# A two-block layer in fp32 on one core: the mixer loop rewritten with 64x64 TensorE tiles, scales in tables, and a planned order for each engine

## What is computed

```
# gated delta rule: 4 heads of 128, the sequence in chunks
kk   = k k^T;   lmat = dec_strict * kk * beta          # strictly lower triangular
sol  = solve(I + lmat, [v, gam * k])                    # unit lower triangular
attn = dec_incl * (q k^T) * beta
# step over the chunks:  u = u_v - w_k S;  o = q_dec S + attn u;  S = g_end S + k_end^T u
o_a  = rmsnorm(o) * gdn_norm_w * silu(z)
# dilated attention: 8 heads of 64, three (window, step) patterns merged into one softmax
p = exp(q k^T + log(number of patterns that hold the pair) - max);  o_b = (p v) / sum(p)
```

## Time and profile before

| what | value |
|---|---|
| time, median of 3 runs | 2759.99 us (2754.16 to 2760.57) |
| time of the profiled execution | 2761.34 us |
| span of its profile | 2759.7 us, granted TensorE clock 0.975 |
| DVE, ACT, POOL busy over the span | 57%, 38%, 6% |
| PE instructions in the mixer loop | 2896 |

### The profile page before, as it was taken

How to read it: one execution, slowest core, us unless ns; L and a number is a source line. 1 busy time by engine, 2 the same in 40 slices (tenths; PEclk the granted TensorE clock), 3 DMA queues, 4 the chain that set the end, 5 groups by cost and what they waited for, 6 DMA issues and landing times.

```text
span 2759.7 us, 33118 instructions
## 1 busy us (share of the span) xinstructions
PE 2632.9 (95%) x12696; PEld 2164.5 (78%) x12696; DVE 1561.2 (57%) x2392; ACT 1060.4 (38%) x1602; POOL 156.2 (6%) x189
## 2 busy tenths in 40 slices
PE   6999979999899999999999999988999999999997
PEld 5878767777777878888878888876888788888886
DVE  4123325555553666666565895456488854755555
ACT  3123323333432453444554444344434333433332
POOL 1000011111220000110000000000000000000000
PEclk9999988999999999999999999999999999999999
DMA  5222230100103445556553456442322333333331
GB/s 193 94 77 87 75 113 16 39 27 27 39 16 107 131 157 192 192 193 203 192 168 92 145 183 191 132 127 69 101 86 89 92 100 92 92 122 99 92 106 62
DMA packets 318304, 304.29 MB, mean 110 GB/s; under 512 B 10207, under 2 KB 277588, under 8 KB 318036
## 3 DMA queue, kind: packets, MB, share of 16 engines
q1 hardware_dynamic: 303188, 244.18, 29.7%
q0 software_dynamic: 14976, 58.20, 5.2%
HBM read 244.68 MB, written 57.67 MB: 110 GB/s over the span
## 4 chain that ended last, share of the span: by engine, by line
PE 84%; DVE 8%; ACT 3%; DMA 2%; issue 2%; SPq 0%; POOLq 0%; POOL 0%; DVEq 0%; ACTq 0%
PE PS L1854 12%; PE PS L1856 12%; PE PS L1855 12%; PE PS L1568 11%; PE PS L1678 7%; PE PS L1871 6%; PE PS L1872 6%; PE PS L1873 6%; PE PS L1786 3%; PE PS L1809 2%; PE PS L1797 1%; DVE wl L1125 1%; ACT wh L796 1%; DVE cg L1515 1%; DMA raw<-in_w_ff 1%
## 5 line engine op out<-in xcount | busy, mean ns | idle before, releaser
L1854 PE MATMUL PS<-hh,wh 128*128 128x512 f32 x1728 | 683.9, 396 | 4.2 <-DVEq L529 2.3
L1856 PE MATMUL PS<-hh,wl 128*128 128x512 f32 x1728 | 673.9, 390 | 0.0
L1855 PE MATMUL PS<-hl,wh 128*128 128x512 f32 x1728 | 673.6, 390 | 0.0
L1125 DVE TENSOR_TENSOR wl<-raw,wh 128x1024 fp32r<-128x1024 f32 x286 | 347.5, 1227 | 393.6 <-ACT wh L796 393.1
L796 ACT ACTIVATE wh<-raw 128x1024 fp32r<-128x1024 f32 x352 | 366.8, 1055 | 517.7 <-PE PS L1873 381.9
L1411 DVE TENSOR_TENSOR x<-x,PS 128x512 f32<-128x512 f32 x432 | 293.0, 684 | 182.7 <-PE PS L1873 181.8
L1854 PEld LDWEIGHTS PS<-hh,wh 128*128 128x128 f32 x1728 | 325.1, 188 | 76.7 <-issue 4.6
L1855 PEld LDWEIGHTS PS<-hl,wh 128*128 128x128 f32 x1728 | 325.2, 188 | 70.9 <-issue 4.6
L1856 PEld LDWEIGHTS PS<-hh,wl 128*128 128x128 f32 x1728 | 325.0, 188 | 68.2
L1871 PE MATMUL PS<-fh,wh 128*128 128x512 f32 x864 | 344.6, 399 | 18.8 <-DVE x L1411 11.0
L1872 PE MATMUL PS<-fl,wh 128*128 128x512 f32 x864 | 340.0, 393 | 0.0
(11 more groups left out here) (290 smaller groups left out, 2921.2 us busy)
## 6 DMA issues: line engine op xcount, KB each, us to landing
raw<-in_w_ff SPq DMA_DIRECT2D x128, 512.0 KB, 3.9
raw<-in_w_up SPq DMA_DIRECT2D x88, 512.0 KB, 4.4
wl_s<-wl POOLq DMA_DIRECT2D x66, 512.0 KB, 5.5
wl<-wl_s SPq DMA_DIRECT2D x66, 512.0 KB, 3.5
raw<-in_w_in SPq DMA_DIRECT2D x60, 512.0 KB, 3.9
raw<-in_w_down SPq DMA_DIRECT2D x44, 512.0 KB, 5.2
raw<-in_w_out SPq DMA_DIRECT2D x32, 512.0 KB, 4.2
qkvz_s<-st POOLq DMA_DIRECT2D x16, 512.0 KB, 2.9
```

The costliest lines, as they stand in the source:

```text
L1125: TTo(wls(slot), raw[:, k % 2], whs(slot).bitcast(F32), ALU.subtract).then_inc(s["w_lo"], 1)
L1854: mm(bank, wh[:, k % 4, cut], hh[:, kk, span(a_)], start=kk == 0, stop=False)
L1855: mm(bank, wh[:, k % 4, cut], hl[:, kk, span(a_)], start=False, stop=False)
L1856: last = mm(bank, wl[:, k % 4, cut], hh[:, kk, span(a_)], start=False, stop=kk == KT - 1)
```

## The change

- The work of the mixer loop is divided differently between turns. A turn c now takes 4 of the 8 query tiles (0, 3, 4, 7 or 1, 2, 5, 6) for both heads of a pair, in six steps (`steps`, `step`) of up to 512 keys each. The heads lie on partitions 0 to 63 and 64 to 127: their scores use rows 0 to 63 and 64 to 127 of the array, with banks 3 and 4, and their product with v writes columns 0 to 63 and 64 to 127 of bank 7. That product is turned round (v stationary with 64 columns, p moving with 128), so the transposed result comes out directly and "heads" goes.
- The transposes of p become matmuls with a diagonal matrix `dgt` that holds 1/sum.
- The inversion works on the two 64x64 diagonal blocks of each head (`both`): levels 0 to 5 have 8 matmuls in "cor" and 16 in "join", all with 64 rows and 64 columns; level 6 has 4 and 4. T and TT lie in one tile `TTT` with one addition for both. Level 0 becomes a level like the others.
- The lengths of q and k and the factors of the decay go into eight tables per chunk instead of four passes over data. They are applied inside other passes, with one DVE instruction for each head (`by_head`) where there was one for four heads. k and q stay as they were loaded, so the transposes "back" go. Three exponentials over the tables are added at the end of phase 1.
- GpSimd does two memsets and nothing else. `ke` and the sum of squares move to ACT (4 instructions each), `qd` and the output's scaling to DVE.
- `ORDER` and the loop over turns go. A class `Mixers` lists every stage with what it waits for and a duration, places them all by a list schedule, and each engine's program is written out in the order of that plan. qkvb and vb get a second buffer.

```
+    TILES = (4, 7, 0, 3), (5, 6, 1, 2)
...
+    BUSY = {"gc": 0.5, "kk": 0.5, "cor": 0.36, "join": 0.6, "cor6": 0.3, "join6": 0.3, "qk": 0.5, "kT": 0.5, "vT": 0.5,
+            "kS": 0.5, "u": 0.5, "o": 1.0, "SU": 0.5, "ot": 0.5, "vt": 1.0,
+            "D": 0.85, "LT": 0.85, "U": 0.38, "T": 0.7, "AT": 0.85, "v": 0.7, "qd": 0.7, "r": 0.85, "St": 0.85, "ov": 0.15, "orec": 0.15,
+            "on": 0.7, "og": 0.76, "lo": 0.7, "mx": 0.3, "dg": 0.7, "blo": 0.25,
+            "gam": 0.6, "E": 0.63, "half": 0.65, "cp6": 0.38, "ke": 0.9, "uc": 0.6, "sq": 1.5, "osd": 2.8, "oh": 0.63,
+            "vb": 1.05, "bhi": 0.25}
...
+    def place(self):
...
+            start = {stage: max(free[engine[stage[0]]], ready_at[stage]) for stage in can}
+            soonest = min(can, key=lambda stage: (start[stage], -left[stage]))
+            e = engine[soonest[0]]
+            near = [stage for stage in can if engine[stage[0]] == e and start[stage] <= start[soonest] + self.NEAR]
+            stage = max(near, key=lambda stage: (left[stage] - self.bias(stage), -rank[stage]))
+            end = start[stage] + self.busy(stage)
...
+        def step(c, j, m):
+
+            return 6 * c + (2 * j + m if j < 2 else 2 + j)
...
             def chunk(c):
+                if c >= 2:
+                    sp.wait_ge(s["og_ready"], c - 1)
                 sp.dma_start(ch[:, c % 2], qkvz_s[:, :, c * P:(c + 1) * P]).then_inc(ch_loaded[c % 2], 16)
...
+            def pair(i):
+                if i >= 2:
+                    sp.wait_ge(s["s_mm"], 12 * (i - 1))
+                sp.dma_start(qkvb[:, i % 2], qkvb_s.rearrange("p (m t) s -> p m t s", m=3)[:, :, i, :]).then_inc(pair_loaded[i % 2], 16)
...
+            nc.gpsimd.memset(G["TTf"][:], 0.0).then_inc(s["consts_set"], 1)
...
-                    if stage == "invert":
...
-                        PT(G["kd"][:], G["knT"][:], G["gam"][:], ALU.mult).then_inc(s["kqd_ready"], 1)
-                        PT(G["qd"][:], G["qnT"][:], G["gam"][:], ALU.mult).then_inc(s["kqd_ready"], 1)
-
-                        pool.wait_ge(s["eb_ready"], c + 1)
-                        PT(G["ke"][:], G["kn"][:], G["E"][:, :, P - 1:P].broadcast_to([P, GH, P]), ALU.mult)\
...
+            act.wait_ge(s["tab_dve"], 4)
+            for dst, src, sign in ((T_NGAM, T_NGC, -1.0), (T_GE, T_GE, 1.0), (T_KE, T_KE, 1.0)):
+                A(tab[:, :, dst:dst + 4], tab[:, :, src:src + 4], ACT.Exp, scale=sign).then_inc(s["tab_act"], 1)
...
+                elif name == "ke":
+                    act.wait_ge(s["kT_mm"], c + 1)
+                    if c:
+                        act.wait_ge(s["su_mm"], c)
+                    for h in range(GH):
+                        last = A(G["ke"][:, h], heads(2)[:, h], ACT.Copy, scale=tab[:, c, T_KE + h:T_KE + h + 1])
+                    last.then_inc(s["ke_ready"], 1)
...
+            TTo(ke, ge, ngc, ALU.add).then_inc(s["tab_dve"], 1)
+            dve.wait_ge(s["tab_act"], 7)
+            done(TS(ngam, ngam, -1.0, None, ALU.mult))
+            done(TTo(ke, ke, tab[:, :, T_BP:T_BP + 4], ALU.mult))
...
+            def by_head(out, in0, col, c, in1, op0, op1):
+
+                for h in range(GH):
+                    last = STT(out[:, h], in0[:, h], tab[:, c, col + h:col + h + 1], in1(h), op0, op1)
+                return last
...
+                elif name == "U":
+                    l = stage[2]
+                    dve.wait_ge(s["lev_l"], 7 * c + l + 1)
+                    if c or l:
+                        dve.wait_ge(s["lev_w"], 7 * c + l)
+                    if l < 6:
+                        TTo(G["U"][:], corner, again(lmask[:, l], GH), ALU.mult).then_inc(s["lev_u"], 1)
+                    else:
+                        TS(G["U"][64:128], corner[64:128], -1.0, None, ALU.mult).then_inc(s["lev_u"], 1)
+                elif name == "T":
...
+                        TTo(G["TTT"][:], G["TTT"][:], inverse, ALU.add).then_inc(s["lev_t"], 1)
...
+                    for e in range(2):
+                        last = TS(dgt[:, j % 2, e], ident[:], ac[:, 3, 2 * j + e:2 * j + e + 1], None, ALU.mult)
...
-                        rows_ = slice(64 * p, 64 * p + 64)
-                        for lo in range(0, n, HALF):
-                            hi = min(n, lo + HALF)
-                            last = mm(PS[:, 3 + lo // HALF, 0:hi - lo], qkvb[rows_, 0, h * P:h * P + P],
-                                      qkvb[rows_, 1, lo:hi], start=True, stop=True)
...
-                                    last = tr(PS[:, 5 + g % 2, b * P:b * P + P],
-                                              sm[:, h % 2, (b0 + b) * P:(b0 + b) * P + P], ident[:])
...
-                                    last = mm(PS[:, 7, 0:64], pt[:, g % 2, b * P:b * P + P],
-                                              vb[:, b0 + b, 64 * p:64 * p + 64], start=b0 + b == 0, stop=b0 + b == h)
...
+            def both(dst, left, right):
+
+                for h in range(GH):
+                    for r in range(2):
+                        q = slice(64 * r, 64 * r + 64)
+                        last = mm(dst(q, h), left(q, h), right(q, h), start=True, stop=True)
...
+                elif name == "cor" and stage[2] < 6:
+                    l = stage[2]
+                    if l == 0:
+                        pe.wait_ge(s["lt_ready"], c + 1)
+                        pe.wait_ge(s["s_ready"], c + 1)
+                    else:
+                        pe.wait_ge(s["lev_t"], 6 * c + l)
+                        pe.wait_ge(s["lev_u"], 7 * c + l)
+                    both(lambda q, h: corner[q, h], lambda q, h: G["LT"][q, h, q],
...
+                    back = (lambda q, h: G["TTT"][q, 1, h]) if l else unity
+                    both(lambda q, h: inverse[q, 0, h], back, lambda q, h: G["U"][q, h])
+                    both(lambda q, h: inverse[q, 1, h], lambda q, h: G["U"][q, h], back).then_inc(s["lev_w"], 1)
...
+                    for e in range(2):
+                        rows_ = slice(64 * e, 64 * e + 64)
+                        last = mm(PS[:, 3 + e, 0:hi - lo], qkvb[rows_, i % 2, 0, at:at + P], qkvb[rows_, i % 2, 1, lo:hi],
...
+                            last = mm(PS[:, 5 + e, b - lo:b - lo + P], soft(j)[:, e, b:b + P], dgt[:, j % 2, e], start=True, stop=True)
...
+                    for b in range(lo, hi, P):
+                        for e in range(2):
+                            ch_ = slice(64 * e, 64 * e + 64)
+                            last = mm(PS[ch_, 7, 0:P], vb[:, i % 2, b // P, ch_], pt[:, e, b - lo:b - lo + P], start=b == 0, stop=b + P == n)
```

More of the change, by code:

```diff
@@ L521, in program @@
         ch_loaded = [sem(f"ch_loaded{i}") for i in range(2)]
-        pair_loaded = sem("pair_loaded")
+        pair_loaded = [sem(f"pair_loaded{i}") for i in range(2)]
         out_moved = [sem(f"out_moved{i}") for i in range(4)]
@@ L540, in rows, with soft @@
             return w[bass.ds(r, P), :]
[L544 to L557, removed]
+        mixers = Mixers()
+        def step(c, j, m):
+            return 6 * c + (2 * j + m if j < 2 else 2 + j)
+        def soft(j):
+            return sm[:] if j % 2 == 0 else raw[:]
         units = [tiles_of(Dense(), b) for b in range(2)]
@@ L624, in _ @@
             chunk(1)
[L625 to L632, removed]
+            pair(1)
+            for c in range(2, TT):
+                chunk(c)
+                if c in (3, 5):
+                    pair((c + 1) // 2)
             end_phase(sp, 2)
@@ L762, in _ @@
-            turns(pool, turn)
             end_phase(pool, 2)
@@ L1378, in _ @@
[L1378 to L1380 removed]
+            ge, ke, ngam, ngc = (tab[:, :, n:n + 4] for n in (T_GE, T_KE, T_NGAM, T_NGC))
+            done(TS(ngc, PS[:, 5, 0:32].rearrange("p (t c) -> p t c", c=4), -1.0, None, ALU.mult))
+            done(V_.tensor_copy(ge, PS[:, 5, 32:64].rearrange("p (t c) -> p t c", c=4)))
+            TTo(ke, ge, ngc, ALU.add).then_inc(s["tab_dve"], 1)
+            dve.wait_ge(s["tab_act"], 7)
+            done(TS(ngam, ngam, -1.0, None, ALU.mult))
@@ L1671, in _, with four @@
                     pe.wait_ge(s["tab_dve"], 3)
-                    mm(PS[:, 5, 0:32], triu[:], tab[:, :, T_G:T_G + 4], start=True, stop=True).then_inc(s["tab_mm"], 1)
+                    mm(PS[:, 5, 0:32], triu[:], tab[:, :, T_G:T_G + 4], start=True, stop=True)
+                    mm(PS[:, 5, 32:64], ones[:], tab[:, :, T_G:T_G + 4], start=True, stop=True).then_inc(s["tab_mm"], 1)
             end_phase(pe, 1)
-            def four(bank, left, right, start=True, stop=True):
+            def four(bank, left, right):
                 for h in range(GH):
-                    last = mm(heads(bank)[:, h], left[:, h], right[:, h], start=start, stop=stop)
+                    last = mm(heads(bank)[:, h], left[:, h], right[:, h], start=True, stop=True)
                 return last
@@ L1950, in _ @@
                     last.then_inc(s["fin_mm"], 1)
-def groups(h):
-    if h < 4:
-        return [(h, h + 1)]
```

(7 more changed lines are left out.)

797 lines of the change are left out of this document (463 added, 334 removed).

## The result

The changed kernel takes 2655.66 us (median of 4 runs, 2653.66 to 2656.01) against 2760.18 us for the kernel before in the same comparison. The ratio is 0.9625, with a 95% interval of 0.9608 to 0.9641: 104 us less. I had forecast 2738 us, 22 less. The time lies inside the range that I gave, but near its low end, 9 us above what I had worked out for the first rival, that quadrants of the array really run at once.

What follows compares the result with a forecast made beforehand. PE was taken as the bound: 51.6 us of work a turn plus 3 of waits, 54.6 against 58.0, saves 27 us over eight turns; edges cost 5, giving 2738 us from 2761.3 profiled. Range 2645 to 2795.

Steps and rivals of the forecast that it cites:

- the first rival: Quadrants of the PE array run at once: inversion 9.4 us, scores 3.9, a turn 43.3, total 2647 us; chance 0.24.
- The bound: Mixer loop: PE's work sets the time, 48.9 us (84%) of a 58.0 us turn before the change.
- The inversion's chain: Dependent steps of one inversion in the loop: 29 us for six levels and 7 more, 36 us, under PE's 51.6.
- The full-tile halves at 0.111 us: Halves of fp32 128x128 matmuls on PE: 64 a turn at 0.111 us, 7.1 us.
- the doubled cost of turning p: Transposes of p become 36 full fp32 matmuls a turn: 8.0 us of PE where there were 4.0.
- The count: Number of PE instructions in the mixer loop after the change: 4416.
- The edges: End of phase 1 (1 us), start of the loop (2) and last turn (2): together 5 us lost.
- the small tiles' price: Inversion on PE: 304 halves of 64x64 matmuls at 0.062 us, 18.8 us a turn where there were 15.1.
- Three slots of four: Scores on PE: the two heads overlap only in part, 5.8 us a turn between 7.7 in line and 3.9 side by side.
- The product with v: 72 halves a turn on PE, heads alternating between column halves, at 0.062 us: 4.5 us; 8.0 in line.
- Nothing overlaps: Rival: scores 7.7, product with v 8.0, inversion 18.8, a turn 60.0 us, total 2781 us; chance 0.14.
- The plan is laid out for other durations: Rival: the plan's durations are too short, waits stay at 9 us, a turn 60.6 us, total 2786 us; chance 0.11.

Runs made afterwards that it cites:

- x1: Changed kernel with the inversion's 64x64 matmuls issued quadrant by quadrant instead of in turn: 2683.2 us, 27.5 more.
- x2: Changed kernel with all key blocks of one head before the other's in the product with v: 2669.4 us, 13.7 more.
- x12: Changed kernel with the scores of both heads of a pair reading rows 0 to 63 of the array: 2681.0 us, 25.4 more.
- x5: Changed kernel with p normalised on DVE and turned by plain transposes, plan laid out again with new durations of dg and tr: 2622.4 us, 33.3 less.
- x4: Changed kernel with only the plan's table of durations replaced by durations from its own trace: 2630.0 us, 25.7 less.
- x3: Changed kernel with a turn's decay placed only after the state of the turn before is written: 2658.3 us, 2.6 more.
- x13: Changed kernel with a turn's decay and scores placed behind the state, scaled output and all attention of the turn before: 2664.1 us, 8.4 more.

## Why the prediction was wrong in size

**What held.** The bound: PE is still 84% of the whole chain, and its lines are some 83% of the chain between 431 and 738 us. Of each PE price that was raised or taken away, most came through to the time: 27.5 of 44 us in x1, 13.7 of 18 in x2, 25.4 of 31 in x12, and 33.3 for 32 in x5. The inversion's chain and DVE stayed under PE. The full-tile halves at 0.111 us and the doubled cost of turning p are as priced, and x5 confirms the latter by taking it away. The count was right: 4416 instructions foreseen, and the loop has 4416 (the window's 4419 hold 11 of phase 3 and miss 8 that start at 394.43). The edges were seen as a loss.

**The step that failed: the small tiles' price, which had no overlap in it.** I charged the inversion's 304 halves 0.062 us each, 18.8 us a turn, by "the row nearest in size", one half after the other. The rows show 0.030 for the 288 that alternate and 0.065 for the 16 of level 6, 9.7 us. For one quadrant on its own the price was about right, 0.058 us measured; what I had left out is that two quadrants run at once. The 8-column transposes of the earlier trace rows all use the same few rows of the array, so they could not show what tiles that alternate do. They also load 128 stationary columns where a small tile loads 64, so that their 0.062 comes close to 0.058 is luck. This term alone is 9.1 us a turn, 73 us in all, of the 106 by which the eight turns gained more than I had foreseen (54.6 us a turn forecast, 41.4 shown).

**The same step in the scores.** "Three slots of four" gave 5.8 us where the rows and x12 show two of four, 3.9. I had reasoned that the halves of one head hold the order of all; the array lets the other head's rows go ahead. The product with v was nearly right, 4.5 charged and 72 x 0.054 = 3.9 shown, but by luck: the 0.062 came from a row without overlap, and 0.054 is half of 0.109.

**The sum as measured**: 7.1 for full matmuls, 1.8 transposes, 8.0 for turning p, 3.9, 3.9 and 9.7 is 34.4 us. The plan's order changes the form of tile 36 times a turn, not 28. At the 0.1 to 0.2 us that the timeline shows (0.56 us from a group of 16 to the next form, 1.09 for eight full halves) this makes some 5 us, and the whole 40 of 41.4 us. I foresaw 51.6 and 3 of waits. PE's waits between 431 and 738 us add to some 16 us in the trace, 2 a turn, and some of the changes of form lie in them.

**The edges were undercharged**, 5 us against 29. I put 2 us on the last turn, which would have little to fill its gaps; it is 17 us more than before, the first turn 12 (3 of them the end of phase 1), and x4 gets 12 of them back by order alone. The two errors go against each other: 106 us too little gain in the turns less 24 too little loss at the edges make the 82 us between 2738 and 2656.

**The rivals.** The first one, quadrants at once, was the case: 43.3 us a turn and 2647 us against 41.4 and 2655.7, close because its turn was too long by 2 us and its edges too short by 24. The Trainium skill (TensorE: Matmul & The Clock Gate, Packing small matmuls) has tiles of different position running at once; x1, x2 and x12 agree: one tile goes at 0.058, 0.109 and 0.43 us a step, and the other tile adds nothing to it where the two alternate. The rule of the Trainium skill (TensorEngine Tiling, Restrictions and Gotchas) that different row tiles cannot access one PSUM bank simultaneously did not hold the inversion back: both quadrants write one bank, on different partitions, at 0.030 us a half against 0.058 in one quadrant. I had let that rule speak for my price, and the measurement decides against it. "Nothing overlaps" is out by x1, x2 and x12. "The plan is laid out for other durations" was true as a mechanism and wrong as a loss against the kernel before: it cost 26 us (x4) of a gain that with x4 is 130.

**What the gain consists of.** x1 and x2 together are 40 us, x12 25, and so much is shown, though the three were not undone together. x1 and x2 undo 7.8 of the 12.1 us a turn that their overlaps hold; if the time follows PE as it did there, the two are worth 40 x 12.1 / 7.8 = 62 us, which is an estimate. Without overlap the small tiles of the inversion would gain nothing: 304 x 0.058 = 17.6 us a turn, against 15.1 for the inversion before. What is left of the 104 us, some 17, is a net of things that pull both ways: for it the transposes that went and the seam between turns with its fallen clock, against it the dearer turning of p (33 us, x5) and the plan for wrong durations (26 us, x4). x3 and x13 show that the pipelining of turns itself is, net, at most 8 us. How the rest splits was not tried.

## What to carry to other kernels

On a PE-bound stage, count how many different tiles the neighbouring matmuls use: two that alternate took half the time here of the same matmuls in one tile (0.030 against 0.058 us a half, 0.054 against 0.109), so a price taken from rows with one tile can be twice too high for them. An edit that only changes their order leaves an overlap at each change of tile: look at single starts, and not at the mean of a group, before calling it undone. A planned order is only as good as its durations: measured ones took 26 us off with no instruction changed. Read the gain over the whole loop, not between two repeated marks in it, because work that lags comes back in the tail.

## What the runs showed of the hardware that I had not expected

- Halves of fp32 64x64 matmuls start 0.030 us apart when two diagonal quadrants alternate, and 0.058 us apart in one quadrant, a diagonal one (x1) or an off-diagonal one (level 6). A half in one quadrant starts ahead of halves in the other that come before it in the program (x1, 580.43 against 580.48).
- Scores with 64 rows for two heads take 1.13 us for four instructions of 512 columns, and 1.98 on the same rows, although the two halves of each head come one behind the other in the program.
- A second engine's SBUF traffic lengthens DVE's passes by kind: with GpSimd busy, an SBUF pass of 685 ns took 874 in the mean and 1.54 us at most, and a pass that reads PSUM stayed at 686.
